# Other columns for the parts of the expert choice in a streaming encoder layer

## What is computed

```
s1 = q[..., :half] . subkeys[:, 0];  s2 = q[..., half:] . subkeys[:, 1]
v1, i1 = top_k(s1, 16);  v2, i2 = top_k(s2, 16)
sc, pos = top_k(v1[:, None] + v2[None, :], 16)
e = i1[pos // 16] * 128 + i2[pos % 16];  g = softmax(sc)
a = gelu(t . u[e]);  out = sum over heads and k of g * a * v[e]
```

## Time and profile before

| | us |
|---|---|
| median of 3 runs | 1808.41 (1806.15 to 1809.05) |
| the profiled execution | 1809.06 |
| its span, first to last instruction | 1807.2 |

### The profile page before, as it was taken

The page is one execution under the profiler, slowest core; times in us unless marked ns, Lnnn a source line. Parts: engine busy times, 40 slices in busy tenths (PEclk is TensorE's granted clock), DMA queues, the critical chain, the costliest instruction groups (busy, mean ns, idle before and its releaser), DMA issues.

```text
span 1807.2 us, 26391 instructions
## 1 busy us (share of the span) xinstructions
PE 1254.0 (69%) x9056; PEld 696.8 (39%) x9056; DVE 1310.1 (72%) x3857; ACT 579.8 (32%) x1995; POOL 527.0 (29%) x569
## 2 busy tenths in 40 slices
PE   8989877678877575788876576679877544434343
PEld 3677532445545232454534233446545111111111
DVE  5563796889666667898766668999666768686754
ACT  2231133333423333333333234343333222222222
POOL 0100232233322322333322323333322433333332
PEclk9989888688898596877899597887998555555555
DMA  6237799999999999999999999999999999999997
GB/s 266 78 95 292 282 414 422 363 425 424 402 423 423 424 423 418 375 396 403 425 423 421 425 422 383 425 389 401 420 423 420 414 427 426 425 427 426 426 416 305
DMA packets 119380, 696.47 MB, mean 385 GB/s; under 512 B 17983, under 2 KB 21118, under 8 KB 49102
## 3 DMA queue, kind: packets, MB, share of 16 engines
q0 software_dynamic: 78848, 570.53, 75.8%
q1 hardware_dynamic: 36686, 121.83, 17.4%
q10 hardware_dynamic: 3712, 2.43, 0.4%
HBM read 691.65 MB, written 3.02 MB: 384 GB/s over the span
## 4 chain that ended last, share of the span: by engine, by line
DMA 31%; DVE 28%; PE 25%; issue 7%; ACT 4%; POOL 1%; ACTq 1%; DVEq 0%; POOLq 0%
DMA rows<-in_peer_uv,index 22%; DVE rows L2646 11%; PE ps_v L1814 6%; PE ps_f L1553 4%; DMA wch<-in_w_row 3%; PE ps_f L1568 3%; DMA wch<-in_w_out 3%; PE ps_h L1794 2%; PE ps_f L1347 2%; DVE score L2322 2%; DMA wch<-in_w_uq 1%; DVE best L2321 1%; PE ps_f L1431 1%; PE ps_f L1471 1%; ACT diag L2158 1%
## 5 line engine op out<-in xcount | busy, mean ns | idle before, releaser
L1324 POOL DMA_INDIRECT rows<-in_peer_uv,index x544 | 517.2, 951 | 1183.1 <-PE ps_v L1814 1004.3
L2646 DVE CUSTOM_DVE_ANT_0 rows<-rows,ps_h 128x1024 f32<-128x1024 f32 x544 | 656.4, 1220 | 269.7 <-DMA rows<-in_peer_uv,index 203.3
L1814 PE MATMUL ps_v<-rows,diag 128*32 128x256 f32 x4352 | 425.1, 507 | 428.0 <-ACT diag L2158 414.7
L1814 PEld LDWEIGHTS ps_v<-rows,diag 128*32 128x32 f32 x4352 | 125.5, 131 | 680.6 <-ACT diag L2158 549.8
L2149 ACT ACTIVATE tan<-arg 128x2 f32<-128x2 f32 x272 | 55.4, 204 | 782.9 <-DVE arg L2656 704.7
L2152 ACT ACTIVATE weight<-tan,lead 128x1 f32<-128x1 f32 x544 | 180.8, 379 | 9.2
L2158 ACT ACTIVATE diag<-sel,weight 128x32 f32<-128x32 f32 x544 | 140.9, 306 | 0.4 <-PE ps_v L1814 0.3
L1553 PEld LDWEIGHTS ps_f<-bufh,wch 128*128 128x128 f32 x768 | 113.6, 232 | 21.2 <-issue 19.0
L1553 PE MATMUL ps_f<-bufh,wch 128*128 128x128 f32 x768 | 119.6, 320 | 0.0
L1347 PE MATMUL ps_f<-wch,bufh 128*128 128x512 f32 (+1 forms) x192 | 84.6, 583 | 22.9 <-DMA wch<-in_w_row 20.7
L1347 PEld LDWEIGHTS ps_f<-wch,bufh 128*128 128x128 f32 x192 | 34.2, 209 | 68.5 <-issue 37.6
(11 more groups left out here) (398 smaller groups left out, 1685.5 us busy)
## 6 DMA issues: line engine op xcount, KB each, us to landing
wch<-in_w_gate SPq DMA_DIRECT2D x60, 512.0 KB
wch<-in_w_row SPq DMA_DIRECT2D x36, 512.0 KB
wch<-in_w_o SPq DMA_DIRECT2D x32, 512.0 KB
wch<-in_w_out SPq DMA_DIRECT2D x24, 512.0 KB
wch<-in_peer_wq SPq DMA_DIRECT2D x24, 512.0 KB
rows<-in_peer_uv,index POOLq DMA_INDIRECT x544
w_tok<-in_w_tok SPq DMA_DIRECT2D x4, 1640.0 KB, 13.7
wch<-in_w_uq SPq DMA_DIRECT2D x6, 384.0 KB
```

The source lines that it names most:

```text
L1324: pool.indirect_dma_start(rows[c % RING][:, :, :].rearrange("p a d -> p (a d)"), None, io.peer_uv[:, :], at).then_inc(s_uv[c % RING], 16)
L1814: ins = nc.tensor.matmul(ps_v[GROUP * a:GROUP * (a + 1), :], diag[:, c % DRING, :], rows[c % RING][:, 1, QD * a:QD * (a + 1)], start=False ...
L2646: v.tensor_tensor_reduce(out=u, in0=u, in1=ps_h[:, :], scale=1.0, scalar=0.0, op0=ALU.mult, op1=ALU.add, accum_out=dots[:, c % KEEP:c % KE ...
```

## The change

The column in which each part of a choice runs is looked up in a table, CHOICES. Block 1 keeps its columns. A tile's first block (blocks 5, 9 and 13) keeps columns 2, 4 ... 22 of the block before. For all others, blocks 2, 3, 4, 6, 7, 8, 10, 11, 12, 14, 15 and 16, the parts run in columns −7, −4, −1, 2, 5, 8, 11, 14, 17, 19 and 22 counted from the start of the block before; −7 is column 25 of the block before that. The last part stays at column 22. ACT's softmax column, the fronts, the gathers and all buffers are as they were.

```diff
--- before.py
+++ after.py
@@ -708,6 +708,7 @@
 NP = len(PASSES)
 CHUNKS = 3 * DC + DC + PH + 1
 PARTS = 11
+AHEAD = (-7, -4, -1, 2, 5, 8, 11, 14, 17, 19, 22)
 NSUMS = 3 + NPAIR + 3 * H
 S_Q = 3 + H + 1
 S_R = S_Q + H
@@ -806,6 +807,25 @@
     share = lambda k: (min(max(k, first_col), last_col) - first_col + 0.001) / (last_col - first_col)
     done = [sum(e <= ends[-1] * share(k) for e in ends) for k in range(SLOTS + 1)]
     return [done[k + 1] - done[k] for k in range(SLOTS)]
+
+
+def choice_columns():
+
+    at = {}
+    for n in range(1, NB):
+        first = SG * (n - 1)
+        for j in range(PARTS):
+            if n == 1:
+                k = CHOICE_AT + j
+            elif BLOCKS[n][1] > 0:
+                k = AHEAD[j]
+            else:
+                k = 2 * (j + 1)
+            at[first + k] = (n, j)
+    return at
+
+
+CHOICES = choice_columns()
 
 
 STEPS = {}
@@ -2683,10 +2703,8 @@
                         dot(b)
                     if b >= 2:
                         next(second, None)
-                    if n == 0 and 0 <= k - CHOICE_AT < PARTS:
-                        choose(1, k - CHOICE_AT)
-                    if 0 < n < NB - 1 and k % 2 == 0 and 1 <= k // 2 <= PARTS:
-                        choose(n + 1, k // 2 - 1)
+                    if b in CHOICES:
+                        choose(*CHOICES[b])
 
 
 class Names:
```

## The result

| | before | after |
|---|---|---|
| median, 20 runs each (us) | 1809.22 | 1815.62 |
| lowest to highest | 1803.11 to 1818.11 | 1808.9 to 1819.94 |
| profiled execution (us) | 1809.06 | 1819.36 |
| its span | 1807.2 | 1817.5 |

The ratio is 1.0036, with a 95% interval of 1.0022 to 1.005, so +6.5 us (+4.0 to +9.0). The forecast of 1808.8 was "no difference"; its range ended at 1815.5, 0.1 under the median. The profiled execution of after lies 3.7 us above its own median, and 3.4 us of its distance to the profile of before are there already when the first column begins (213.79 against 210.44), in a part of the program that is not changed. What follows compares lengths of stretches, not moments.

The account below looks back on a forecast made before the run. Bound: stretches where DMA engines move under 424 GB/s because DVE consumes late. Terms −3.0 (blocks 1 and 2), +1.7 (blocks 4 to 6) and +1.7 (blocks 8 to 10) sum to +0.4 us: 1808.8 us, range 1801 to 1815.5.

Parts of the forecast that it names:

- A: DMA dip at 311.9 to 357 us, blocks 1 and 2, losing 6.4 us; forecast to fall to 5.75.
- B: DMA dip at 450 to 461 us, losing 2.3 us; forecast to be back at 424 GB/s.
- C: DMA dip at 712 to 737 us, losing 5.7 us; forecast to lose 10.8 after the change.
- s: How much later DVE reaches a place than before; grows by parts moved ahead of it, falls by parts moved behind.
- rival 3: Slower TensorE clock in the gates at 1110 to 1125 us: +3.9 us, 1812.3 us; chance 0.05.
- F: DMA dip at 1110 to 1125 us, losing 4.1 us; forecast to lose 7.5 after the change.
- E: DMA dip at 807 to 858 us, losing 2.3 us; loss summed from 712 us forecast at 12.6, before 10.9.
- D: DMA dip at 737 to 802 us, losing 2.9 us; loss summed from 712 us forecast at 11.3, before 8.6.
- G: DMA dip at 1187 to 1215 us, losing 3.6 us; loss summed from 1110 us forecast at 11.1 or 13.8.
- Rival 1: TensorE and ScalarE set the heads' chains, so moved parts cost nothing there: −8.3 us, 1800.1 us; chance 0.27.
- Rival 2: Each dip counts for itself, a delayed one not sparing the next: +5.3 us, 1813.7 us; chance 0.18.
- Rival 4: Gathers unaffected, index complete at column 22 as before, shifts end inside the rings: stays at 1808.4 us; chance 0.10.

Follow-up runs that it names:

- five parts: Against the kernel before, only parts 0 to 4 of block 6 moved, to columns 25, 26, 28, 30 and 31 of block 4: ratio 1.0045, +8.1 us.
- the tail alone: Against the kernel before, new columns only for blocks 14, 15 and 16: ratio 1.0012 (0.9995 to 1.003), +2.2 us.

## Why the prediction was wrong

**What bounds the kernel: right, as far as tested.** Time is lost where the DMA engines move less than 424 GB/s: the heads in which they moved 303 to 329 made slower kernels, the one in which they moved 422 the fastest. As a sum over one profile it is coarse (+6.2 us where +6.5 was measured, with the scatter told above).

**Pass 1, −3.0: agrees, but is not shown.** A loses less, B is at 419 GB/s, and blocks 2 to 4 alone gave −2.9. But that interval holds nothing too, and the 5.6 us that the pass lost lie within the 4.5 to 9.6 of kernels that leave pass 1 alone.

**Pass 2, +1.7: the step that failed.** Blocks 6 to 8 alone gave +6.7 us (+3.6 to +9.8). Two things were wrong in it, and they were of different weight.

The first is the size of C. The ledger had s = 5.1 there and a level of 10.8; it lost 13.4 in its wider cut (5.9 before), 7.5 more. The chain from oab to the first index score became 6.4 us longer, and 5.1 of that are the three parts. The other 1.2 can be followed: DVE's arguments of the pair of columns ahead of the transposes end 5.1 us later in the chain, and ScalarE's copy yo, ahead of its copy kt of the transposes, comes 6.3 us later. Between them lie TensorE's transposes. TensorE in that stretch, before and then after (busy us, granted clock, DMA share, GB/s):

```profile
712.30:715.80 3.50, 3.50 (x28) 0.71 1.02 413
```

```profile
719.40:724.10 4.70, 4.70 (x28) 0.50 0.94 373
```

The same 28 matmuls took 4.70 us at a granted clock of 0.50 (1.2 GHz) instead of 3.50 at 0.71 on average. This is rival 3's mechanism, in C and not in F, where the gates took 2.05 us as before. It is given back further on: the second index product and the gates of C ran at the faster clock, the gates in 2.05 us instead of 3.78. So the clock does not explain the loss. The Trainium skill (TensorE: Matmul & The Clock Gate, HAM oscillation) says that idle stretches bring the slow clock back. Right before the mixes that precede these transposes TensorE stood idle for 1.52 us, against 0.61 in before; but the other traces don't bear out that this idle time is the cause. After the same 1.5 us the stretch took 3.9 us with blocks 6, 7 and 8 alone and 4.4 with block 6 alone, and with five parts it took 4.7 after 0.54.

The second, and larger, is the assumption that s is back at +1.0 "when all of block 6's parts are done", so that DVE makes good what the head cost it. DVE can't take back its lateness by having less to do: between the dips it is at once behind the gathers, which are late themselves. The rows at 757.94 and 764.58 show it, and measured from column 24 of block 4, column 20 of block 5 and column 0 of block 6 both lie 6.0 us later than before, where the ledger had +1.0. In the profiles of the other four kernels with block 6 in the head, column 0 of block 6 is 2.8 to 6.9 us later. In columns 6 to 31 of block 5 the dots waited 1.6 to 5.1 us for gathers in these five kernels, and not at all in before. With s = 6 at E the ledger's own rule (the highest level counts) gives 10.9 + 6 = 16.9 for the pass; it lost 17.1. So the rule was not what failed, but the s put into it. Where the loss falls behind C is not steady: in after D vanished (2.8 to 0) and E grew (2.3 to 3.7), and so with blocks 6 to 8 alone; in the other three D kept 1.0 to 2.0 us and E 1.7 to 2.9. Five parts in place of three showed the same with a larger dose: +8.1 where a ledger that expects DVE to catch up gives +2.3.

**Pass 3, +1.7 as the middle of +0.4 and +3.1: the trace looks like the upper reading, but the size is not shown.** F lost 8.1 (forecast level 7.5), G took the total to 13.9 (11.1 or 13.8 forecast), H vanished. The pass lost 3.2 more than before, and the prediction's own text had the reason, "gathers that are themselves late leave s": the waits at 1149.24 and 1162.89 stand where the one of 0.79 us was in the earlier trace rows. What was seen as a possibility in pass 3 should have been applied to pass 2.

The size of this term is known less well than that of pass 2: blocks 10 to 12 alone gave +2.2 us (−1.3 to +5.6), and kernels that leave pass 3 alone lost 10.9 to 19.4 us in its head and rest, in which after lost 15.9.

**The tail, nothing: right,** by the 345.5 and 346.1 us above. Block 14's dots still wait for gathers, 15.4 us against 14.4 in the earlier trace rows:

```profile
L2666 DVE CUSTOM_DVE_ANT_0 rows<-rows,ps_h 128x1024 f32<-128x1024 f32 x32 | 38.8, 1220 | 18.2 <-DMA rows<-in_peer_uv,index 15.4 <-PE ps_h L1814 1.9 <-issue 0.5
```

**The rivals.** Rival 1 (not late where it lands) fell with the longer heads. Rival 2 (losses add up, gains don't carry) comes nearest: +5.3 forecast, +6.5 measured, and the sign by which it was to decide, DVE waiting for gathers between two dips of a pass, is in the trace. Its places were not all right: it had D grow by 1.7 us and E vanish, and it was D that vanished and E that grew. The sum is right in part by luck. Rival 3's sign, gates in F at 3.8 us, did not come (2.05). Rival 4 fell too: the index is complete at column 22 as before, and yet pass 2 got slower.

**What stays open.** Why blocks 6 and 10 with less work for DVE in the rests of their passes give nothing at all, and not a little, is argued from the rates (413 of 424 GB/s leave at most 7.3 us in the rest of pass 2, in dips set by other steps), not tried. Block 7's +2.7 us is within its interval of nothing. The sizes of the terms of pass 1 and pass 3 stay open, as said above.

## What to carry to other kernels

Where a ring of transfers is fed by an engine that also does other work, find the stretches in which that engine's order of work is a chain to the next release, here the three heads. Work put into such a chain was paid in full (the second head grew by 1.0 to 1.2 us for each us), and work taken out of the rest of the pass gave almost nothing back, since there the consumer is already as early as its gathers. So don't spread work evenly over columns: put it where the engine waits for others ahead of the chain, in this kernel the 7.5 us before the first head (−7.2 us of time with three parts of one block), and stop when the transfers in the chain run at their full rate.

In a ledger of lateness, an engine that waits for transfers catches up only down to the moment its next transfer lands. The Trainium skill (Perfetto Trace Analysis, Optimization Strategy) says that the most contended engine can change over the regimes of a kernel and that one may interleave regimes. The traces agree as to the change, 380 GB/s in the heads against 411 to 416 in the rests, and add that moving work from one regime to the other has to go by which of them is at its bound.

## What the runs showed of the hardware

The same 28 matmuls of transposes and mixes took 3.50 us at a mean granted clock of 0.71 and 4.70 us at 0.50, in kernels that differ by parts of DVE work. The idle time right before them does not tell which it will be: it was 1.5 us in four kernels, with 3.9, 4.4, 4.7 and 4.7 us for the stretch, 0.5 with 4.7, and nothing at all with 4.1 to 4.2 in the two kernels that have only block 2 early.

The third head can be slow with no instruction in it changed. In the kernel with block 7 alone it took, and likewise in the one with five parts of block 6 (39.25 us, 0.54):

```profile
1094.47:1133.71 39.24, 23.21 (x120) 11.14 (x117) 30.17 (x81) 14.65 (x41) 11.71 (x12) 0.54 0.86 344
```

In before it was 34.08 us long at a granted clock of 0.70, with TensorE busy 16.91 us for the same 119 or 120 matmuls, as the rows of the heads show. The first gate after this head took 3.78 us in those two kernels and 2.05 in before. In the kernel with the tail alone the head was 36.19 us and the gate 3.19. In the other nine kernels that leave pass 3's head alone, before among them, it was 33.4 to 34.6 us at clocks of 0.64 to 0.75. So up to 5 us of this head can go with the clock, as much as with three parts of DVE work. The 37.5 and 37.7 us with blocks 10 to 12 moved, at 0.64, are not explained so, since at 0.64 and 0.65 unmoved heads took 33.4 to 34.6. What made the clock stay low in the three slow ones was not found.
